# Gates and query tokens spread over the partitions by TensorE instead of by copies through DRAM, in a one-core layer kernel

## What is computed

```
# first block, experts: each token picks 128 of 16384 experts
h2 = rms_norm(x, ffn_norm_g)
eidx, gate = top experts of h2            # (256, 128) indices and weights
u, v = expert_u[eidx], expert_v[eidx]     # two rows of 1024 floats per token and expert
act = gelu(einsum('tnd,td->tn', u, h2)) * gate
x = x + einsum('tn,tnd->td', act, v)
h3 = rms_norm(x, ple_norm_g)
x = x + sigmoid(h3 @ w_ple_gate) * (p @ w_ple_proj)

# second block
mod = silu(c) @ ada_w + ada_b             # sh1, sc1, g1, sh2, sc2, g2
hc = modulate(rms_norm(ctx, norm1_g), csh1, csc1)
_, ctx_states = mixer_block(hc, ...)      # needs ctx and the lora weights only
out_x, _ = mixer_block(modulate(rms_norm(x, norm1_g), sh1, sc1), ..., ctx_states)
x = x + g1 * out_x
x = x + g2 * conv_ffn(modulate(rms_norm(x, norm2_g), sh2, sc2))
return rms_norm(x, final_g)
```

## Time and profile before

| what | us |
|---|---|
| median of 3 runs | 1628.71 (1627.07 to 1630.46) |
| the profiled execution's own time | 1626.22 |
| its span in the trace | 1624.4 |
| start and end of the rows (first dot product, last matmul) | 347 to 1028 |
| busy: PE, DVE, ACT, POOL | 1201.1, 932.0, 421.6, 339.8 |
| moved by DMA | 412.34 MB |

### The profile page before, as it was taken

One profiled execution on the slowest core, in us unless ns is written; L12 is line 12 of the kernel. 1 busy time (PEld: TensorE's weight loads), 2 busy tenths in 40 slices (PEclk: granted clock), 3 DMA queues, 4 the chain that ended last, 5 costly groups with the idle time before them and its releaser, 6 DMA issues.

```text
span 1624.4 us, 26294 instructions
## 1 busy us (share of the span) xinstructions
PE 1201.1 (74%) x11106; PEld 819.1 (50%) x11106; DVE 932.0 (57%) x2059; ACT 421.6 (26%) x1060; POOL 339.8 (21%) x315
## 2 busy tenths in 40 slices
PE   7989888963484433447747766579987877999997
PEld 6468773850152100115514442257887853888843
DVE  2977664555986888795677656221445343455501
ACT  3011400012432322453363332223242300111100
POOL 1000011114453344444546453000000000000000
PEclk9998998985597555569868887699999999999999
DMA  9552388799999999999999999424200023344441
GB/s 371 187 182 90 106 290 293 243 363 336 421 415 343 407 421 415 417 414 418 419 418 420 420 419 419 152 78 156 104 9 4 4 106 104 117 154 149 150 148 73
DMA packets 112295, 412.34 MB, mean 254 GB/s; under 512 B 10648, under 2 KB 35744, under 8 KB 78896
## 3 DMA queue, kind: packets, MB, share of 16 engines
q0 software_dynamic: 44576, 297.35, 45.2%
q1 hardware_dynamic: 63360, 106.48, 19.2%
q10 hardware_dynamic: 4240, 6.83, 1.9%
HBM read 408.51 MB, written 2.12 MB: 253 GB/s over the span
## 4 chain that ended last, share of the span: by engine, by line
PE 52%; DMA 26%; DVE 10%; ACT 6%; issue 3%; POOL 2%; ACTq 0%; POOLq 0%; DVEq 0%
PE psum L500 25%; DMA arena<-in_experts,arena 24%; PE psum L510 7%; PE psum L1691 5%; PE psum L2175 5%; DVE arena L1270 3%; PE psum L1301 3%; POOL arena L1257 2%; PE psum L596 1%; ACT arena L1281 1%; PE psum L2059 1%; PE psum L719 1%; ACT arena L1286 1%; DMA arena<-in_lora_up 1%; DMA weights<-in_w_att_out 1%
## 5 line engine op out<-in xcount | busy, mean ns | idle before, releaser
L1301 PE MATMUL psum<-arena 128*32 128x512 f32 x1024 | 194.5, 846 | 295.8 <-ACT arena L1286 292.5
L500 PE MATMUL psum<-actT,weights 128*128 128x256 f32 x1824 | 401.3, 382 | 5.2 <-ACT actT L613 2.3
L1257 POOL DMA_INDIRECT arena<-in_experts,arena x256 | 309.9, 1211 | 402.1 <-PE psum L1301 324.4
L500 PEld LDWEIGHTS psum<-actT,weights 128*128 128x128 f32 x1824 | 348.7, 192 | 56.9 <-ACT actT L613 5.6
L1301 PEld LDWEIGHTS psum<-arena 128*32 128x32 f32 x1024 | 23.8, 126 | 401.8 <-ACT arena L1286 373.9
L1270 DVE CUSTOM_DVE_ANT_0 arena<-arena 128x1024 f32<-128x1024 f32 x96 | 116.8, 1223 | 58.7 <-DMA arena<-in_experts,arena 57.9
L1270 DVE CUSTOM_DVE_ANT_0 arena<-weights,arena 128x1024 f32<-128x1024 f32 x96 | 117.2, 1224 | 54.6 <-DMA arena<-in_experts,arena 52.8
L1276 ACT ACTIVATE arena<-arena 128x2 f32<-128x2 f32 x128 | 26.0, 203 | 401.4 <-DVE arena L1270 401.3
L1270 DVE CUSTOM_DVE_ANT_0 arena<-normed,arena 128x1024 f32<-128x1024 f32 x64 | 77.3, 1226 | 37.6 <-DMA arena<-in_experts,arena 36.7
L1691 PE MATMUL psum<-arena 64*64 64x64 f32 (+1 forms) x2816 | 82.3, 227 | 15.0 <-DVE arena L1808 7.1
L1691 PEld LDWEIGHTS psum<-arena 64*64 64x64 f32 x2816 | 78.5, 139 | 23.0 <-issue 11.5
(11 more groups left out here) (354 smaller groups left out, 1607.8 us busy)
## 6 DMA issues: line engine op xcount, KB each, us to landing
weights<-in_w_in SPq DMA_DIRECT2D x18, 2048.0 KB, 8.6
arena<-in_ada_wT POOLq DMA_DIRECT2D x48, 512.0 KB, 6.0
weights<-in_ffn_w_up SPq DMA_DIRECT2D x22, 1024.0 KB, 6.5
weights<-in_ffn_w_down SPq DMA_DIRECT2D x5, 2048.0 KB, 7.7
weights<-in_w_out SPq DMA_DIRECT2D x4, 2048.0 KB, 12.9
weights<-in_w_peer_q SPq DMA_DIRECT2D x4, 2048.0 KB, 10.6
arena<-in_experts,arena POOLq DMA_INDIRECT x256, 13.5
weights<-in_w_ple_gate SPq DMA_DIRECT2D x2, 2048.0 KB, 10.4
```

Of the source, the lines that this page charges most:

```text
L500: mm = nc.tensor.matmul(out[:, c * T:(c + 1) * T], w[:, k, c * P:(c + 1) * P], act[:, k, :], start=(k == 0), stop=(k == kc - 1))
L1257: nc.gpsimd.indirect_dma_start(out=rows[:, n % RING, :], out_offset=None, in_=dram["experts"], in_offset=bass.IndirectOffsetOnAxis(ap=eidx ...
L1301: mm = nc.tensor.matmul(SUMS[sum_part(k, i), i, :], diag[:, pos, :], rows[:, pos, D + 512 * i:D + 512 * (i + 1)], start=first, stop=last, ...
```

## The change

Four things are rewritten.

- The loads of `lora_up` and `ctx` leave ACT. SP issues them in a new `sp_ctx`, ahead of tile `ctx_lora` in its list, with the same waits. The stages `act_modulation` and `act_ctx_load` are gone.
- The gates no longer go through DRAM. Two pieces at the end of `pe_ple_proj` multiply `modT`'s column, broadcast over 128 columns, with the identity: eight 128 x 128 matmuls for each gate. ACT copies the two results to `gatebc`. The two stores and the load of 1 MB are gone, and `beside` gets 4 pieces of `ple_proj` in place of 3.
- The quads of block 1: SP loads block 1's 128 query tokens once, 128 partitions x 4 KB (`sp_last_tokens`). TensorE spreads them with columns of the identity (`pe_quads`, four pieces behind `scan_common`, 8 matmuls of 128x32 by 128x512 each), ACT copies each quad from PSUM (`act_quads`, 128x1024).
- ACT runs one gelu on a single column, behind the exp of the first `select`, ahead of its wait for the last query product.

```diff
@@ sp_weights
+                if name == "ctx_lora":
+                    sp_ctx(sp)
                 if name == "ple_proj1":
-                    sp_quad_tokens(sp)
+                    sp_last_tokens(sp)
@@
-        def sp_quad_tokens(sp):
+        def sp_last_tokens(sp):
             sp.wait_ge(S("normed_out"), 16)
-            src = normed_rows[P:2 * P].rearrange("(g t) d -> t g d", g=QUADS)
-            for j in range(QUADS):
-                part = slice(QP * j, QP * (j + 1))
-                sp.dma_start(quad_ring[part], src[:, 0:QUADS - 1, :]).then_inc(S("quad_in0"), 16)
-                sp.dma_start(quad_last[part], src[:, QUADS - 1, :]).then_inc(S("quad_in1"), 16)
+            sp.dma_start(quad_last, normed_rows[P:2 * P]).then_inc(S("last_tokens"), 16)
+
+        def pe_quads(pe):
+            pe.wait_ge(S("last_tokens"), 16)
+            pe.wait_ge(S("ckk_dve"), 3)
+            for g in range(QUADS):
+                if g >= 2:
+                    pe.wait_ge(S("quads_cp"), g - 1)
+                for i in range(2):
+                    for j in range(QUADS):
+                        mm = nc.tensor.matmul(G[g % 2][QP * j:QP * (j + 1), 512 * i:512 * (i + 1)],
+                                              K("ident")[:, QP * g:QP * (g + 1)], quad_last[:, 512 * i:512 * (i + 1)],
+                                              start=True, stop=True)
+                        if i == 1:
+                            mm.then_inc(S("quads_pe"), 1)
+                yield
+
+        def act_quads(act):
+            product(act, "ctx_v")
+            for g in range(QUADS):
+                act.wait_ge(S("quads_pe"), QUADS * (QUADS if g == QUADS - 1 else g + 1))
+                nc.scalar.copy(quad_row(1, g), G[g % 2]).then_inc(S("quads_cp"), 1)
+                yield
@@ act_queries
                 if i == 2:
                     for _ in act_select(act, 0, 0):
                         pass
+                    nc.scalar.activation(gelu[:, 0, 0:1], K("eps"), ACT.Gelu_apprx_tanh)
@@ act_ple_proj
-            act.wait_ge(S("cdone"), 1)
-            act.wait_ge(S("gate_out"), 32)
-            act_load(act, "gate", gatebc.rearrange("p g n -> p (g n)"),
-                     gate_rows.rearrange("g n -> (g n)").partition_broadcast(P))
-            yield
+            for g in range(2):
+                act.wait_ge(S("gatebc_pe"), g + 1)
+                nc.scalar.copy(gatebc[:, g, :], gate_bank(g)).then_inc(S("gatebc_ok"), 1)
+                yield
@@ pe_ple_proj
+            pe.wait_ge(S("mod_ok"), 1)
+            for g, first in enumerate((2 * DC, 5 * DC)):
+                wait_freed(pe, f"ple_proj{g}")
+                for c in range(DC):
+                    mm = nc.tensor.matmul(gate_bank(g)[:, c * P:(c + 1) * P],
+                                          modT[:, first + c, 0:1].to_broadcast([P, P]), K("ident"), start=True, stop=True)
+                mm.then_inc(S("gatebc_pe"), 1)
+                yield
@@
-        def act_modulation(act):
-            wait_freed(act, "mix_out1")
-            act_load(act, "lora", loraup, dram["lora_up"].rearrange("d p n -> p d n"))
-            act.wait_ge(S("mod_ok"), 1)
-            for g, first in enumerate((2 * DC, 5 * DC)):
-                act.dma_start(gate_rows[g].rearrange("(c p) -> p c", p=P), modT[:, first:first + DC, 0],
-                              allow_slow_non_contiguous=True).then_inc(
-                    S("gate_out"), 16)
-
-        def act_ctx_load(act):
-            act.wait_ge(S("sc_pe"), QUARTERS * TB)
-            act_load(act, "ctx", ctok, dram["ctx"].rearrange("(b p) d -> p b d", p=P))
+        def sp_ctx(sp):
+            wait_freed(sp, "mix_out1")
+            act_load(sp, "lora", loraup, dram["lora_up"].rearrange("d p n -> p d n"))
+            sp.wait_ge(S("sc_pe"), QUARTERS * TB)
+            act_load(sp, "ctx", ctok, dram["ctx"].rearrange("(b p) d -> p b d", p=P))
@@
-        stage(act=act_modulation)
-        stage(act=act_ctx_load)
@@
+        early.append(dict(pe=pe_quads, act=act_quads, pieces=QUADS))
@@
-        beside += [dict(pe=pe_ple_proj, act=act_ple_proj, pieces=3)]
+        beside += [dict(pe=pe_ple_proj, act=act_ple_proj, pieces=4)]
```

More of the change, by code:

```diff
@@ L527, in toks @@
             return ps[:, :].rearrange("p (b n) -> p b n", b=TB)
-        ACT_LOADS = ("lora", "ctx", "pT", "gate", "gup", "fg")
+        ACT_LOADS = ("lora", "ctx", "pT", "gup", "fg")
         def act_load(act, name, dst, src):
@@ L1263, in dve_group @@
             if isinstance(t, int) and t == 0 and g < 2:
-                for half in (g,) if b == 0 else range(2):
-                    dve.wait_ge(S(f"quad_in{half}"), 16 * QUADS * (b + 1))
+                if b:
+                    dve.wait_ge(S("quads_cp"), QUADS)
+                else:
+                    dve.wait_ge(S(f"quad_in{g}"), 16 * QUADS)
             for k, pos, n, filled in turn_slots(b, t, g * GROUP, count):
@@ L1357, in pe_ple @@
             turned(pe, "n3")
+            pe.wait_ge(S("gatebc_ok"), 2)
             for i in range(2):
@@ L1383, in pe_ple_proj, with gate_bank @@
                 yield
[L1387 to L1400 removed]
+            pe.wait_ge(S("mod_ok"), 1)
[6 more added lines that the diff above has]
+                yield
+        def gate_bank(g):
+            return G[tile_at[f"ple_proj{g}"] % 2]
+        NORMS = dict(x1=(0, 0, 0, "norm1_g"), ctx=(1, 0, 1, "norm1_g"), x2=(2, 3 * DC, 0, "norm2_g"))
+        def sp_ctx(sp):
[3 more added lines that the diff above has]
+            act_load(sp, "ctx", ctok, dram["ctx"].rearrange("(b p) d -> p b d", p=P))
         def act_ctx_norm(act):
@@ L1549, in pe_direction @@
                     pe.wait_ge(S(t + "kk_dve"), 3)
+                    pe.wait_ge(S("quads_cp"), QUADS)
             elif m.apart:
@@ L2145, in add_gated @@
         def add_gated(dve, st, name, gate_, temps):
-            dve.wait_ge(S("act_load"), act_loaded("gate"))
+            dve.wait_ge(S("gatebc_ok"), 2)
             for i in range(2):
```

1 line of the change is left out of this document (removed).

## The result

Measured beside each other on one chip, the kernel before took 1629.59 us (median, 1627.07 to 1631.26) and the changed one 1611.69 us (1608.31 to 1613.70), four executions each. The ratio is 0.9891, 95% interval 0.9865 to 0.9917. The forecast was 1605, its range 1599 to 1615: the time is in the range, but 6.7 us above the forecast. A gain of 23.5 us was expected and 17.9 us came.

What follows compares the result with a forecast made beforehand. DMA gathers at 418 GB/s were taken to bound the rows, plus two holes. Terms 8.9 + 8.3 + 6.3 = 23.5 us off a median of 1628.7 gave 1605 us, range 1599 to 1615.

Steps and rivals of the forecast that it cites:

- The rows' length: DMA-bound gathers of the rows: bytes over 418 GB/s plus two holes, to become 23.5 us shorter in all.
- The first hole: 363 to 376 us at 131 GB/s: ACT's wait for lora_up delays POOL's ninth gather; closing it gains 8.9 us.
- The fourth rival: Another hidden wait still holds ACT at the front: 14.6 us less gain, 1614 us; chance 0.03 for 1608 to 1616.
- The second hole: 506 to 532 us at 284 GB/s: block 1's copies onto 32 partitions are slow; removal gains 8.3 us, or 6.2.
- Bytes: In the saturated rows, copies and gates' broadcast go, one load comes: net 2.62 MB at 418 GB/s, 6.3 us.
- TensorE's additions at nothing: Beside the rows, added matmul sets and ACT copies fit into turns of 5.0 us under queued gathers: cost 0.
- the other end of 17.6 us: The cost if all added TensorE matmuls and ACT copies came onto the rows' loop: 7.8 + 3.9 + 6 x 0.99.
- the 41 us of slack: Between SP's issue of last_tokens and TensorE's first set of quads, 41 us are left for 1 MB.
- The context: Loads moved behind ctx_v: ctx lands at 399.8 us, before its norm needs it; the rival, landing late and slower, 0.04.
- From there to the end 600 us are untouched: Everything behind the rows' end stays as long as before, 600 us, so no term was given to it.

Runs made afterwards that it cites:

- The loads alone: Kernel before with only the loads of lora_up and ctx moved to SP's queue; 1629.52 us against 1631.88, ratio 0.9987.
- the gates alone: Kernel before with only the gates spread by TensorE, no single floats or broadcast load; one execution, 1625.26 us beside a median of 1633.49.
- Wide copies alone: Kernel before with block 1's eight copies onto 128 partitions instead of 32, same bytes, tokens not rearranged; one execution, 1621.15 us beside 1633.49.
- the quads alone: Kernel before with only block 1's query tokens spread by TensorE; 1621.74 us against 1631.88, ratio 0.9933.
- 48 more: Kernel before plus 48 repeated small TensorE matmuls, as many as the change adds, run twice; first 1633.80 us, ratio 1.0003.
- 64 more: Kernel before plus 64 repeated small TensorE matmuls, beside 1631.67 us for the kernel before; rows 692.8 us, 605.3 us behind them.
- 16 more: Changed kernel plus 16 repeated small TensorE matmuls, run twice; 1608.12 us, ratio 0.9858 to the kernel before, then 1608.5, ratio 0.9869.

## Why the prediction was right where it was, and where it failed

**The rows' length: right in sum.** 23.5 us were forecast. The five traces of the kernel before with its own transfers (two as they are, three with matmuls added) have 692.7 us on average (691.7 to 694.0), and the five with all of the change 668.0 to 668.6, 668.3: 24.4 us. The parts alone give 12.5 (quads), 10.5 (gates) and 1.5 (loads), and 24.5 together, so they add up. In medians the change gained 17.9, 17.6 and 21.6 us on three chips, so 3 to 7 us of the 24.4 do not arrive; see the last two points.

**The first hole: the amount right, the cause wrong.** The 8.9 us were "filled" by an earlier ninth gather: "I take 8.9, since data in the queue, not the moment of issue, is what fills it." That step failed. The loads alone had the early gather and the queued data and kept the loss, 8.9 us spread over 60; the gates alone had the late gather and won 8.0. The prediction had the right suspect in its hands: the single floats, "some 9 us of all engines" by queue q10's 32.0% in the earlier trace rows. It called that a thing that "matters too", beside a wait on the chain, when it was most of the price. The amount was luck, though: the floats' own packets, added up in the trace, took 3.8 us of all engines in the kernel before and 1.2 us in the loads' run, which still lost 8.9; most of q10's share belonged to its two loads. Busy DMA engines at 131 GB/s are the sign: they were not idle, and single floats were under way. ACT's wait alone leaves 3.4 us of hole in the gates' run, and taking it away alone gained 1.5 in the loads' run. The forecast came out because the change removes both. The sentence behind it, that the floats would have taken turns with the gathers had they stayed, fits the loads' run. The fourth rival (ACT still starts late) was mispriced for the same reason: it was given a gain of 14.6 us, but gates and quads, each measured alone and with ACT late, add up to 23.0 of the 24.5.

**The second hole: right, and for the stated reason.** 8.3 us were taken, with 6.2 as the other end if reading were slow. Wide copies alone gave 7.8, and the stretch went from 284 to 415 GB/s. The row had it open; the Trainium skill's page "SBUF — State Buffer", section "Door 1: The DMA port swizzle", decided for the destination, and the runs agree with it. With the quads replaced, bytes (2.10 less 0.52 MB, 3.8 us) and hole make 12.1, and 12.5 were measured.

**Bytes: right.** 409.73 MB moved, 412.34 before: 2.61 less, for 2.62.

**TensorE's additions at nothing: right in the rows, their size right by luck.** A set of quads took 1.92 us, and 1.94 were estimated. But the row behind the estimate, x8 in the earlier trace rows, is four matmuls of the program at a granted clock of 0.5 (the text before the prediction calls them eight, too), and a set of quads is eight, x16. So the estimate at that clock should have been 3.9 us a set; 1.92 came because the clock stood at 1.00 there, where the rows' own four took 1.06. The same holds for the gates' sets (x16 in 2.05 us), and the other end of 17.6 us should have been 29. It did not matter, since a turn is 5 us: the quads alone shortened the rows by 12.5 us where bytes and hole make 12.1. Small matmuls did nothing to the rows either: 692.4 and 692.5 us with 48 more, 692.8 with 64, 691.7 and 694.0 without. last_tokens landed 14.5 us after its issue at 491.71, and TensorE came to its first set at 536.73 with 0.37 us of idle time, put down to VectorE, so the wait cost nothing, as the 41 us of slack said:

```profile
arena<-normed_rows SPq DMA_DIRECT2D x1, 512.0 KB, 14.5
```

**The context: right.** SP's in-order wait for lora_up pushed the issue of ctx to 384.70 us, 34.4 behind lora_up's at 350.28 (40.6 in the loads' run; 12.0 us to landing in ACT's queue). The estimate had the same moment at 347.2 + 26.0 + 12.0 = 385.2. The norm did not notice; the chain goes through ACT's own work, answering to the earlier trace rows:

```profile
414.43 0.42 ACT arena L1308 x2
414.86 1.04 ACT arena L557 x2
```

The forecast had put the norm at 412.

**"From there to the end 600 us are untouched": the step that failed.** 23.5 forecast less 17.9 measured leaves 5.6 us. Apart from two waits for the gates' copies, no instruction behind the rows was changed, and the time there was not the same: 606.9 to 609.2 us in three traces, 599.3 and 601.8 in the two of the kernel before. The forecast had no term for the clock there. Shown is that 4 us of such a difference come and go with the granted clock in one stretch of 46 us, in executions with the same TensorE program; that the stops move with the number of matmuls; that the solves are 3.2 us longer on average with the stop at 32; and that on one chip the kernel before lost 4.0 us with 48 more matmuls (ratio 1.0010 to 1.0030) and nothing with 64 more, 4.2 us between these two. On the other chip 48 more showed no loss (0.3 us). Open is how much of it the 48 added matmuls cause in the changed kernel. 16 more gained 7 to 10 us behind the rows in the profiled executions, but that is in part the pick: all three profiled executions of the changed kernel were the longest of their set, and both with 16 more the shortest. In medians the kernel with 16 more gained 25.4 us on one chip, where the changed one did not run, and 1.6 us more than it on the chip where both ran, which the intervals don't tell apart.

**The head, not foreseen either.** To the first gather it is 331.6 to 334.0 us in the four traces where TensorE's work is unchanged, 333.1 to 338.6 in the others, and 335.8 to 338.6 for the changed kernel. The code ahead of the rows is the same but for the early gelu of one column. Five of the traces with more matmuls have no early gelu (gates alone, quads alone, 48 more twice, 64 more) and stand at 333.1 to 336.5 us, so the gelu is not all of it. The head differs between executions of one kernel too (331.6 and 333.4; 335.8 to 338.6), and no run took it apart. The changed kernel without the early gelu was not tried, so its own share stays open.

## What to carry to other kernels

Where the DMA engines are shown busy and the rate is low, look first for who puts the small or narrow pieces into the queues (single floats, 32 partitions), and price them by the rate that is lost, not by their queue's share of the engines (2.0% of 40 us here, beside 8.9 us lost); a wait on the chain at the same place may be a neighbour of the cause. Test by keeping one and removing the other: here the loads alone and the gates alone turned the attribution round. And in a stage that TensorE bounds, "untouched" has to be read from more than one trace of each kernel, with the granted clock beside it: cut the traces at the same two instructions, and look at where the profiled execution stands among all of its kernel, before anything is credited.

The best version of those run is the changed kernel with 16 redundant matmuls, 1608.1 and 1608.5 us, 23 to 25 us (ratios 0.9858 and 0.9869) under the kernel before; on the one chip that ran both, it was not told apart from the changed kernel.

## What the runs showed of the hardware

- 2048 stores of one float each cost about 8 us of transfer time at 418 GB/s (8.0 by the rows' length without them, 8.9 by the rate beside gathers), though their own packets took 3.8 and 1.2 us of all engines. They landed after 22.2 us beside two loads and after 46.1 beside gathers.
- Transfers onto 32 partitions slow down the whole stream around them: 284 GB/s for 26 us with 2.1 MB of them, 415 with the same bytes onto 128 partitions, and 7.8 us less of rows.
- TensorE's stops of 0.3 to 2 us, waiting for nothing that the profile shows, stand at places 256 records (matmuls and weight loads) apart, at some of these places and not at others, and their place in the program moves with the number of instructions ahead. The Trainium skill's page "Advanced Engine Details and Errata", section "ISA Cache", gives a line of 16 KB as 256 instructions. The traces agree in size: from 1196 to 1240 us in the kernel before, TensorE has 2624 records, and the only transfers are ten of 16 KB in queue q8, one for 262 records. That a stop is the wait for such a transfer is not shown by any run here.

```profile
1196.00:1240.00 44.00, 37.69 (x1312) 36.35 (x1312) 25.17 (x31) 18.70 (x29) 0.00 (x0) 1.00 0.01 4
...
q8 instruction: 10, 0.16, 1.4%
```

- The same 244 matmul records took 45.7 us at a granted clock of 0.96 and 49.8 at 0.88, and one kernel can have either.
- A load behind 2 MB in the same queue held up the next issue for 34 us (41 in the loads' run), where its own queue had landed it in 12.0.
